# Recurrent pairs: the inverse's turned form by a product and masked copies in place of transposes, head rows spread by one fp32r product

## Reference

```
kk = kk / max(sqrt(sum(kk * kk over a head)), 1e-12)
S_t = S_{t-1} diag(w_t) + (S_{t-1} a_t) b_t^T + v_t k_t^T      a = -kk, b = kk * rate
y_t = S_t r_t
yn  = (y - mean) * rsqrt(var + GN_EPS)                          per head
out = ((yn * g + b + bonus) * gate) @ w_out
```

## Time and profile before

| | |
|---|---|
| three executions | 3204.98, 3205.87, 3208.65 us |
| the profiled execution's own time | 3205.82 us |
| its span, first to last instruction | 3204.0 us |
| mean granted TensorE clock | 0.998 |
| TensorE matmul busy | 3145.8 us, 98% |
| VectorE busy | 2132.3 us, 67% |
| ScalarE busy | 1459.1 us, 46% |
| rv2's first unit ends, about | 2481 us |
| the pair loop, about | 2495 to 2690 us |
| the chain and the head norms, about | 2690 to 2733 us |

### The profile page before, as it was taken

How to read it: one execution, slowest core, us unless ns; L and a number is a source line. 1 busy time by engine, 2 the same in 40 slices (tenths; PEclk the granted TensorE clock), 3 DMA queues, 4 the chain that set the end, 5 groups by cost and what they waited for, 6 DMA issues and landing times.

```text
span 3204.0 us, 52305 instructions
## 1 busy us (share of the span) xinstructions
PE 3145.8 (98%) x22626; PEld 2696.1 (84%) x22626; DVE 2132.3 (67%) x2715; ACT 1459.1 (46%) x1993; POOL 136.3 (4%) x134
## 2 busy tenths in 40 slices
PE   9999999999999999999999999999999999999998
PEld 7887787888889988988899887998777777799886
DVE  6546766775389835363898458995666655799637
ACT  3357644443255523432555345554336564355424
POOL 2100000000000001000100011000120000100002
PEclk9999999999999999999999999999999999999999
DMA  5311232232323223222232332322223000133331
GB/s 183 115 53 66 91 107 80 92 102 90 105 86 106 96 98 114 95 88 92 84 102 97 106 105 80 106 102 91 85 81 103 16 4 16 66 106 106 105 100 65
DMA packets 47236, 287.03 MB, mean 90 GB/s; under 512 B 6416, under 2 KB 6688, under 8 KB 21408
## 3 DMA queue, kind: packets, MB, share of 16 engines
q1 hardware_dynamic: 44960, 279.51, 25.6%
q0 software_dynamic: 2048, 4.20, 0.5%
HBM read 277.39 MB, written 2.10 MB: 87 GB/s over the span
## 4 chain that ended last, share of the span: by engine, by line
PE 80%; DVE 5%; ACT 2%; issue 1%; POOL 0%; DVEq 0%; ACTq 0%
PE ps L527 42%; PE ps L2850 8%; PE ps L2872 7%; PE ps L2871 7%; PE ps L2870 7%; PE ps L4192 3%; PE ps L4230 1%; PE ps L1251 1%; DVE wl L344 1%; ACT wh L328 1%; PE ps L1252 1%; PE ps L1253 1%; DVE xl L3666 0%; PE ps L3282 0%; DVE tmp L3674 0%
## 5 line engine op out<-in xcount | busy, mean ns | idle before, releaser
L344 DVE TENSOR_TENSOR wl<-raw,wh 128x2048 fp32r<-128x2048 f32 (+2 forms) x215 | 434.2, 2020 | 328.4 <-ACT wh L328 328.1
L527 PE MATMUL ps<-xl,wh 128*128 128x512 f32 (+1 forms) x1312 | 503.6, 391 | 3.0 <-POOL xl L3563 3.0
L328 ACT CAST wh<-raw 128x2048 fp32r<-128x2048 f32 (+2 forms) x212 | 356.9, 1683 | 292.0 <-PE ps L527 263.7
L527 PE MATMUL ps<-xh,wh 128*128 128x512 f32 x1056 | 416.5, 395 | 13.0 <-DVE xl L3666 3.4
L527 PE MATMUL ps<-xh,wl 128*128 128x512 f32 x1056 | 390.2, 392 | 0.2 <-DVE wl L344 0.2
L527 PEld LDWEIGHTS ps<-xl,wh 128*128 128x128 f32 (+1 forms) x1312 | 245.8, 187 | 56.7 <-POOL xl L3563 3.8
L527 PEld LDWEIGHTS ps<-xh,wh 128*128 128x128 f32 x1056 | 197.8, 187 | 66.2 <-issue 16.3
L527 PE MATMUL ps<-hid_r,wh 128*128 128x512 f32 x640 | 249.0, 389 | 0.0
L527 PEld LDWEIGHTS ps<-xh,wl 128*128 128x128 f32 x1056 | 197.5, 187 | 44.6 <-issue 1.0
L2870 PE MATMUL ps<-terms_h,sums_h 128*128 128x256 f32 x768 | 217.3, 283 | 0.0
L2871 PE MATMUL ps<-terms_l,sums_h 128*128 128x256 f32 x768 | 217.3, 283 | 0.0
(11 more groups left out here) (570 smaller groups left out, 7720.1 us busy)
## 6 DMA issues: line engine op xcount, KB each, us to landing
raw<-in_up SPq DMA_DIRECT2D x88, 1024.0 KB, 4.9
raw<-in_down SPq DMA_DIRECT2D x64, 704.0 KB, 4.0
raw<-in_up_c SPq DMA_DIRECT2D x22, 1024.0 KB, 4.9
raw<-in_down_c SPq DMA_DIRECT2D x16, 704.0 KB, 4.0
raw<-in_gates SPq DMA_DIRECT2D x8, 1024.0 KB, 4.8
raw<-in_gv SPq DMA_DIRECT2D x8, 1024.0 KB, 4.8
raw<-in_gu SPq DMA_DIRECT2D x8, 1024.0 KB, 4.8
raw<-in_gout SPq DMA_DIRECT2D x8, 1024.0 KB, 4.9
```

What stands on the lines that cost most here:

```text
L328: nc.scalar.copy(wh[:, slot, 0:w], raw[:, slot, 0:w]).then_inc(hi_ready, 1)
L344: nc.vector.tensor_tensor(wl[:, slot, 0:w], raw[:, slot, 0:w], wh[:, slot, 0:w].bitcast(F32), ALU.subtract).then_inc(lo_ready, 1)
L527: last = nc.tensor.matmul(out, stationary, moving, start=(fresh and q == 0), stop=(t == kt - 1 and half == per - 1 and q == 2), skip_group ...
```

## The change

Levels 1 to 4 have no transposes any more. At level 0 X is turned once, as before. After `dx` of level n a further product `dt` forms the turned addition from the same two operands with their parts exchanged, into the bank of the turned X; it reads by_feature and writes by_feature. VectorE copies it into the turned X where a turned mask is set (`add_turned`, a new COPY_PREDICATED behind each `add_x` of levels 1 to 4). ScalarE's four copies of the turned X go. `z` at level n now waits for `add` of level n - 1, `dx` for `turned` of level n - 1. z of level 4 stands ahead of `tokens_v`, behind `ends_r`.

The spreads become one fp32r product. Its 0/1 table picks two rows of a head: row 0 gets the number rounded to fp32r (`highs`, with the sign turned in row 1) and row 1 the rest. `split_rows` makes them with two vector instructions: once on 128 x 512 for the keys' norms, five times on 128 or 64 columns for the roots. The table is copied to fp32r once (128 x 256). The three instructions for the norms stand in the vector engine's lead, and both spread(0) and the lead itself wait for them (count 6 of `kn_norm`, where it was 3). Two more DMAs fetch the turned masks and the kinds of rows.

```diff
-        tail[:, (n + 1) * P:(n + 2) * P] = row == 16 * n + 8 * head
+        tail[:, (n + 1) * P:(n + 2) * P] = (row // 8 == 2 * n + head) & (row % 8 < 2)
...
+    wm += [s % 8 == 1, np.where(s % 8 == 1, -1.0, 1.0)]
...
-        for s, n in ((kn_square, KD), (kn_sum, 1), (kn_norm, 3)):
+        for s, n in ((kn_square, KD), (kn_sum, 1), (kn_norm, 6)):
...
+        def split_rows(dve, steps, done, exact, highs, rows_r):
+            dve.wait_ge(steps.sem, done)
+            nc.vector.tensor_scalar(highs, exact, high_sign, None, ALU.mult).then_inc(steps.sem, 1)
+            dve.wait_ge(steps.sem, done + 1)
+            return nc.vector.scalar_tensor_tensor(rows_r, exact, low_row, highs.bitcast(F32), ALU.mult, ALU.add)
...
+            def add_turned(m, n):
+                need(dve, pB, m, f"dt{n}")
+                mark(nc.vector.copy_predicated(blocks(xt_), where_turned(n - 1), blocks(ps[:, bank["xt"], :])), vB, f"turned{n}")
...
                 masks_here(dve)
+                split_rows(dve, kn_norm, kn_norm.base + 3, key_norms[:, :], key_highs[:, :],
+                           key_norms_r[:, :]).then_inc(kn_norm.sem, 1)
+                picks = const[:, CONST["pick_low"]:CONST["pick_high"] + P]
+                nc.vector.tensor_copy(picks_r[:, :, :].rearrange("p n c -> p (n c)"), picks).then_inc(kn_norm.sem, 1)
+                dve.wait_ge(kn_norm.sem, kn_norm.base + 6)
                 sum_decays(0)
...
                 add_x(m, 1)
+                add_turned(m, 1)
                 bonus(m)
                 add_x(m, 2)
+                add_turned(m, 2)
...
                 add_x(m, 3)
+                add_turned(m, 3)
...
                 add_x(m, 4)
+                add_turned(m, 4)
...
-                mark(nc.tensor.matmul(ps[:, bank["spread"], :], table("pick_low" if m < 4 else "pick_high")[rows, :],
-                                      key_norms[rows, :], start=True, stop=True), pS, "spread")
+                mark(nc.tensor.matmul(ps[:, bank["spread"], :], picks_r[rows, m // 4, :],
+                                      key_norms_r[rows, :], start=True, stop=True), pS, "spread")
...
+                else:
+                    need(pe, vB, m, f"add{n - 1}")
                 products(pB, f"z{n}", feature_half("z"), (by_token, ab, by_token, xs_[m % 2]))
 
             def dx(m, n):
                 need(pe, aB, m, f"z{n}")
+                if n > 1:
+                    need(pe, vB, m, f"turned{n - 1}")
                 products(pB, f"dx{n}", token_half("dx"), (by_feature, xt_, by_feature, z_))
+
+            def dt(m, n):
+                products(pB, f"dt{n}", lambda e, c: by_feature(ps[:, bank["xt"], :], e, c), (by_feature, z_, by_feature, xt_))
...
-                pe.wait_ge(kn_norm.sem, kn_norm.base + 3)
+                pe.wait_ge(kn_norm.sem, kn_norm.base + 6)
                 spread(0)
...
                 dx(m, 1)
+                dt(m, 1)
                 if behind:
                     ends_x(m - 1)
-                xt(m, 1)
                 z(m, 2)
...
                 if behind:
                     ends_r(m - 1)
+                z(m, 4)
                 if ahead:
                     tokens_v(m + 1)
-                xt(m, 3)
-                z(m, 4)
-                if ahead:
                     tokens_k(m + 1)
                     tokens_a(m + 1)
...
-                nc.vector.reciprocal(inverse[:, at_], inverse[:, at_]).then_inc(c_inverse.sem, 1)
+                nc.vector.reciprocal(inverse[:, at_], inverse[:, at_]).then_inc(kn_norm.sem, 1)
+                split_rows(dve, kn_norm, kn_norm.after(b, 1), inverse[:, at_], inverse_highs[:, at_],
+                           inverse_r[:, at_]).then_inc(c_inverse.sem, 1)
```

More of the change, by code:

```diff
@@ L3855, in rwkv @@
         vA = Named(sem("grams_vector"), ["x0", "rb_t", "ak_t", "rk_t", "bonus"], KD, lead=True)
-        vB = Named(sem("levels_vector"), ["add1", "add2", "add3", "add4", "add5"], KD, lead=True)
+        vB = Named(sem("levels_vector"), ["add1", "turned1", "add2", "turned2", "add3", "turned3", "add4",
+                                          "turned4", "add5"], KD, lead=True)
         vC = Named(sem("ends_vector"), ["r_new", "m"], KD, lead=True)
@@ L3859, in rwkv @@
         aA = Named(sem("grams_scalar"), ["eye", "k_v", "b_a", "ab", "akv"], KD, lead=True)
-        aB = Named(sem("levels_scalar"), ["xt0", "z1", "xt1", "z2", "xt2", "z3", "xt3", "z4", "xt4", "z5"], KD, lead=True)
+        aB = Named(sem("levels_scalar"), ["xt0", "z1", "z2", "z3", "z4", "z5"], KD, lead=True)
         aC = Named(sem("ends_scalar"), ["new", "n", "y0"], KD, lead=True)
@@ L3863, in rwkv @@
         pS = Named(sem("spread_tensor"), ["spread"], KD, lead=True)
-        pB = Named(sem("levels_tensor"), ["xt0", "z1", "dx1", "xt1", "z2", "dx2", "xt2", "z3", "dx3", "xt3", "z4", "dx4", "xt4", "z5",
+        pB = Named(sem("levels_tensor"), ["xt0", "z1", "dx1", "dt1", "z2", "dx2", "dt2", "z3", "dx3", "dt3", "z4", "dx4", "dt4", "z5",
                                           "dx5"], KD, lead=True)
@@ L4111, in z, with turned_x @@
                 mark(nc.scalar.activation(of_chunks(z_), in_halves("z"), ACT.Copy), aB, f"z{n}")
-            def turned_x(m, n):
-                need(act, pB, m, f"xt{n}")
-                if n == 0 and m:
+            def turned_x(m):
+                need(act, pB, m, "xt0")
+                if m:
                     need(act, pB, m - 1, "dx5")
-                mark(nc.scalar.copy(xt_, ps[:, bank["xt"], :]), aB, f"xt{n}")
+                mark(nc.scalar.copy(xt_, ps[:, bank["xt"], :]), aB, "xt0")
             def ends(m):
@@ L4378, in pair_tensor @@
                 dx(m, 4)
+                dt(m, 4)
                 if ahead:
@@ L4612, in spread @@
                 rows = slice(32 * (m % 4), 32 * (m % 4) + 32)
-                nc.tensor.matmul(ps[:, self.bank(m), :], table("pick_low" if m < 4 else "pick_high")[rows, :], inverse[rows, :],
+                nc.tensor.matmul(ps[:, self.bank(m), :], picks_r[rows, m // 4, :],
+                                 inverse_r[rows, :],
                                  start=True, stop=True).then_inc(self.spread_out.sem, 1)
```

39 lines of the change are left out of this document (22 added, 17 removed).

## The result

Four executions of the changed kernel took 3226.01 to 3230.46 us, median 3227.68; four of the kernel before, beside them, had a median of 3206.32. The ratio is 1.0069, 95% interval 1.0057 to 1.0081. The profiled execution took 3227.25 us against 3205.82 before: +21.4 us, where the prediction had +9.3 and an upper end of 3221.

What follows compares the result with a forecast made beforehand. The prediction took the tensor engine's queue, busy for 98%, as the bound. Lead-in +7.1, loop +5.3 and chain and tail -3.1 gave +9.3 us on 3205.82, so 3215.1 us, range 3207.5 to 3221.

Steps and rivals of the forecast that it cites:

- the loop's sum: Pair loop: tensor work and new waits over all pairs add 5.3 us, bounds +1 and +10.
- part 1: Levels 1 to 4 of the loop: dt costs 0.90 us as a diagonal product, +3.6 us per pair.
- third rival: Loop: dt runs in quarters its neighbours leave free, at 0.51 us, giving 12.5 us back, 3202.6; chance 0.08.
- Part 2: Levels 1 to 4 of the loop: the transposes go, -2.6 us of tensor work per pair; their scalar copies cost nothing.
- Part 3: Loop: one fp32r spread of 0.25 us replaces two passes of 1.05 us, -0.82 us for each of seven.
- Part 4: Within a pair: masked copies in the vector queue bring new tensor waits, together 0.5 us, bounds 0 and 1.2.
- the first of the three waits: Level 4 of a pair: z4 waits 0.1 us for add3, delayed behind the chain to operand_k.
- second rival: Loop: the vector queue becomes the bound, a pair loses 2 us more, 3227 us in all; chance 0.10.
- Its own sign: Loop, for the vector queue as bound: a pair over 24 us with tensor waits on masked copies.
- Part 5: Lead-in, rv2 units 0 to 1: spread(0) waits for the split, +5.1 us, lower clock +2.0, together +7.1 us.
- first rival: Lead-in: no stall, the vector engine reaches the split before unit 0 ends, 3208 us; chance 0.08.
- Part 6: Chain and tail: root splits add 0.4 us ahead of the first spreads, later spreads save; together -3.1 us.

Runs made afterwards that it cites:

- e4: The changed kernel with the key norms split early and dt as 8 products of 128 columns in place of 16 of 64: 3211.47 us.
- e6: The changed kernel with ten unused fp32 matmuls put into the tensor engine's wait ahead of spread(0): 3226.16 us.
- e9: As e6, with 13 in place of 10 in keep_busy ahead of spread(0): 3224.05 us.
- e8: The kernel before the change with an unread dt behind dx at levels 1 to 4, transposes kept, no vector work added: 3233.66 us.
- e2: The changed kernel with the key norms split early and levels 1 to 4 transposed as before, fp32r spreads kept: 3203.89 us, ratio 0.9993 to the kernel before.
- e10: As e2, with the inverted roots split once over 512 columns in place of five small splits: 3204.10 us, ratio 0.9994 to the kernel before.

## Why the prediction was wrong

**Sign right, size wrong.** "Slower" had a chance of 0.70; the profiled time lies 12.2 us above the forecast and 6.2 above the range.

**The step that failed** is the loop's sum, "+5.3 us, bounds +1 and +10". It priced each step by its slot and each wait by its semaphore, and had no term for the supply of instructions. Outside the stretches the loop takes 210.0 - 9.5 = 200.5 us, before 195.2 - 1.5 = 193.7: +6.8, within 1.5 us of the forecast. The stretches add 8.0. By the finer count at the seams (11.7 and 2.1 us) it is +5.3 outside and +9.5 at the seams; that the first is the forecast itself to a tenth is partly luck, since its terms were off both ways (below). The sign of it stood in the trace of before: two idle stretches marked `issue`, and a number of instructions that the change raised from 11056 to 12866, which the sum of part 1 turned into microseconds only. That the seams are the cause is shown by e4 (half of dt's instructions, 5 stretches, the waits for VectorE unchanged), by the distances in multiples of 256, and by the packets: only seams reached soon after their packet's start stall. Two more runs bear on it. The matmuls that e6 and e9 put ahead of the loop moved the seams against the loop's code, by 40 and 52 instructions; other places stalled, and there were again 10 stretches, of 9.9 and 10.0 us. So no fixed place in the code does it. What sets the start of a packet stays open, and no run slowed the fetches themselves.

Part by part:

- **Part 1, dt: right.** 0.88 us from e8, forecast 0.87 to 0.93. The diagonal form was the right row to price it by, and the third rival (0.51 us) fell. It is 1.7 times the 0.51 us of a product on four quarters, not twice; and a dt of 1.02 us would have cost 32 x 0.12 = 3.8 us more over the run than one of 0.90, where the prediction says 3.
- **Part 2, the transposes: not separable.** The +6.8 us outside the stretches (5.3 by the finer count) hold it together with parts 1, 3 and 4.
- **Part 3, the spread: mis-sized.** The forecast took the 0.25 us of matmuls that follow one another in rout; one lone fp32r product between quarter products holds the queue for 0.43. Its saving is so 0.62 us and not 0.82 (1.05 less 0.25 would have been 0.80), seven times 0.20 us or 1.4 us less in the loop. What made up for it by the finer count is not shown. And e2 shows a second thing that it missed: with the transposes kept, 0.41 us of the gain turn into xt2's wait for add2.
- **Part 4, the waits in a pair: mechanism right, size not separable.** add3 starts at 2591.82, 3.2 us behind turned2's start (2588.60), behind the operand instructions as forecast. But the waits for VectorE sum to 5.4 us where they were 5.8; they did not grow by 0.5 a pair. The products' waits on add (L4023, 2.6 us) took the place of those of transposes and products on add before (L4002, 2.5 us), and none is for turned (L4027). By its own numbers the first of the three waits was nothing: add3 ends at 2579.45 + 0.73 = 2580.2, when TensorE wants z4, not at 2580.3. The second rival (the vector queue becomes the bound) came out near the measured time, 3227, by luck: its reason is not there. Its own sign, more than 2 us a pair of tensor waits on masked copies, is missing.
- **Part 5, the lead-in: mechanism right, the sum exact by some luck.** Forecast 5.1 for the wait and 2.0 for the clock; measured 5.67 (unit 1 at 2488.01), less the 0.12 by which unit 0 ended later, and 1.56 (14.12 less 12.56; e9 against e6 gives 1.66). The wait so came out 0.45 us longer and the clock 0.44 cheaper. Unit 1 starts 0.6 us later than the 2487.4 of the forecast: 0.2 are the start of the spread (2487.32, forecast 2487.1), 0.4 the spread itself, 0.69 us at the lower clock where 0.3 was reckoned. The first rival (no stall) fell.
- **Part 6, the chain: mis-sized.** Forecast +0.4 ahead of the first head spread, measured +1.8. It counted the last pair of splits only. VectorE is without a pause from 2732.60 on, and four of the five splits stand in that stretch, 0.5 to 0.7 us each. e10 got 0.8 of it back by one wide split. Behind it spreads 5 to 7 saved 2.91 against 3.54 us each, 0.6 and not 0.82, the same lone slot as in part 3. Together -0.7, forecast -3.1.

The sum with what was measured: 7.1 + 6.8 + 8.0 - 0.7 = 21.2 us (or 5.3 + 9.5 for the two in the middle), with 0.1 by which unit 0 ended later 21.3, against 21.4.

## What to carry to other kernels

Count a change's instructions on the busiest queue as well as its microseconds: where it puts a dense block of small matmuls in the place of a few wide ones, look at idle time that no semaphore explains and at its distance in instructions, and prefer the form with fewer instructions even if its slot is the same. A packet of instructions that starts 2 us or less before its block is wanted is the sign to look for. When an engine waits in order, ask where a new instruction stands on the other engine's queue; three instructions of 1.5 us in the wrong `between` cost 7 us. And a shorter matmul that leaves idle time behind may cost the clock: fill the wait, or it gives back the gain.

## What the runs showed of the hardware

- TensorE's instructions arrive in packets of 16 KB, one for 256 of them. At 57 instructions a microsecond two of 43 seams held the engine up for over 0.5 us; at 63.8 to 64.8, nine to eleven of 50, for 0.5 to 1.9 us each.
- Behind such a stretch the first instruction came 2.2 to 2.9 us after the packet's start, in all fourteen kernels. In the changed kernel the seams reached within 1.8 us of it stalled, the others were reached after 2.0 us or more.
- A product's slot of 0.86 to 0.88 us for 16 quarter-array fp32 matmuls on the diagonal did not depend on 32 or 64 columns, nor on 16 of 64 or 8 of 128.
- The granted clock fell behind 1.44 us of idle time although 4.48 us of matmuls stood ahead of it, and did not fall behind 0.15 us. Behind 0.87 and 1.47 us around the head spreads it fell in one kernel (e10, 0.62) that differs little from one where it did not (e2, 0.35 and 1.46 us), in one profiled execution of each.
